# Weight slabs ahead of constants at the start, and the next sample's keys turned in one place, in a hybrid streaming step on one core

## What is computed

```
proj = h @ w_in                         # q, k, v, and the indexer's qi, ki, wi
logits = q @ keys.T * ATTN_SCALE + bias + mask      # 512 cached keys and 16 new ones
probs = softmax(logits)
out = probs @ vals                      # 16 heads, 4 key heads, head size 64
x = x + out @ w_o
```

## Time and profile before

| | us |
|---|---|
| median of 3 runs | 1809.35 (1809.22 to 1810.82) |
| the profiled execution, its own time | 1810.91 |
| its span in the profile | 1809.1 |
| TensorE busy (matmul row) | 1786.6 |
| VectorE busy | 1313.3 |
| ScalarE busy | 825.8 |
| GpSimd busy | 348.8 |

### The profile page before, as it was taken

One profiled execution on the slowest core, in us unless ns is written; L12 is line 12 of the kernel. 1 busy time (PEld: TensorE's weight loads), 2 busy tenths in 40 slices (PEclk: granted clock), 3 DMA queues, 4 the chain that ended last, 5 costly groups with the idle time before them and its releaser, 6 DMA issues.

```text
span 1809.1 us, 35107 instructions
## 1 busy us (share of the span) xinstructions
PE 1786.6 (99%) x13025; PEld 1692.4 (94%) x13025; DVE 1313.3 (73%) x2450; ACT 825.8 (46%) x1477; POOL 348.8 (19%) x381
## 2 busy tenths in 40 slices
PE   8999999999999999999999999999999999999998
PEld 7887668999999999999999999998999999999998
DVE  5498976468576677978788888888535756758786
ACT  4223875334343433536545655456333434334353
POOL 0002663200000000123333343422020100000011
PEclk9999999999999999999999999999999999999999
DMA  6372144333343343233444334444323433334232
GB/s 162 75 121 66 61 135 136 97 87 88 90 95 91 77 111 77 69 79 108 140 138 141 105 122 124 145 139 153 119 81 97 97 94 82 100 82 97 77 84 76
DMA packets 326708, 186.27 MB, mean 103 GB/s; under 512 B 39536, under 2 KB 319184, under 8 KB 325552
## 3 DMA queue, kind: packets, MB, share of 16 engines
q1 hardware_dynamic: 307904, 173.49, 34.1%
q0 software_dynamic: 15840, 7.87, 3.5%
q10 hardware_dynamic: 2832, 3.15, 0.5%
HBM read 164.30 MB, written 19.99 MB: 102 GB/s over the span
## 4 chain that ended last, share of the span: by engine, by line
PE 81%; DVE 3%; ACT 1%; issue 1%; DVEq 0%; ACTq 0%
PE psum L1452 26%; PE psum L203 26%; PE psum L1517 19%; PE psum L621 1%; PE psum L625 1%; PE psum L572 1%; PE psum L585 1%; PE psum L2759 1%; PE psum L554 0%; PE psum L597 0%; PE psum L608 0%; DVE WL L195 0%; PE psum L2730 0%; PE psum L2743 0%; PE psum L566 0%
## 5 line engine op out<-in xcount | busy, mean ns | idle before, releaser
L203 PE MATMUL psum<-b2H,WH 128*128 128x320 f32 x896 | 213.7, 320 | 1.2 <-DVE b2L L1250 0.7
L1517 PE MATMUL psum<-HH,HT 128*128 128x320 f32 x680 | 210.4, 309 | 0.8 <-DVE xT L1731 0.4
L1517 PE MATMUL psum<-HL,HT 128*128 128x320 f32 x680 | 210.7, 310 | 0.0
L203 PE MATMUL psum<-b2H,WL 128*128 128x320 f32 x896 | 204.1, 309 | 0.0
L203 PE MATMUL psum<-b2L,WH 128*128 128x320 f32 x896 | 203.8, 308 | 0.0
L1452 PE MATMUL psum<-b2H,HT 128*128 128x320 f32 x816 | 186.1, 309 | 0.0
L1452 PE MATMUL psum<-b2L,HT 128*128 128x320 f32 x816 | 186.1, 309 | 0.0
L191 ACT ACTIVATE WH<-W 128x1024 fp32r<-128x1024 f32 x89 | 94.0, 1056 | 194.3 <-PE psum L203 180.8
L1517 PE MATMUL psum<-HH,LT 128*128 128x320 f32 x560 | 173.5, 310 | 0.0
L203 PEld LDWEIGHTS psum<-b2H,WH 128*128 128x128 f32 x896 | 146.3, 188 | 11.2 <-issue 8.4
L1452 PE MATMUL psum<-b2H,LT 128*128 128x320 f32 x672 | 153.1, 309 | 0.0
(11 more groups left out here) (437 smaller groups left out, 4203.2 us busy)
## 6 DMA issues: line engine op xcount, KB each, us to landing
W<-ssm_w_in SPq DMA_DIRECT2D x96, 256.0 KB, 3.1
RW<-mlp_w_up SPq DMA_DIRECT2D x64, 256.0 KB, 3.0
RWx<-mlp_w_up SPq DMA_DIRECT2D x64, 256.0 KB, 3.2
RW<-mlp_w_down SPq DMA_DIRECT2D x64, 256.0 KB, 3.1
RWx<-mlp_w_down SPq DMA_DIRECT2D x64, 256.0 KB, 3.2
bc<-scratch_acs SPq DMA_DIRECT2D x8, 1280.0 KB, 7.7
W<-attn_w_in SPq DMA_DIRECT2D x32, 256.0 KB, 3.8
prev<-state_ssm SPq DMA_DIRECT2D x16, 512.0 KB, 5.3
```

The lines of the kernel that those rows point to most:

```text
L203: last = pe.matmul(psum[0:m, b.out + h, 0:TH], w[:, b.slot, k, 0:m], r[:, k, h * TH:(h + 1) * TH], start=(n == 0 and i == 0), stop=(n == K ...
L1517: last = pe.matmul(down_bank(g, i), w[:, k], x[:, DNB[i], k], start=(opens and k == 0 and c == 0), stop=(k == 3 and c == 2), skip_group_ch ...
```

## The change

It has two parts. On SyncE's queue the loads of slab 0 and slab 1 move up behind the first two small loads, then the queue waits until the last column group of the tokens has landed (`x_in[3]`), and only then issues the constants that stood around the slabs.

In the sample streams half 1 of the keys leaves its place between the two halves of the probabilities of step b - 1, and is turned right behind half 0, at the end of step b - 2. It uses bank 5 in place of bank 6, and waits for the copy of the turned probabilities that lay there (`ptn`). VectorE's copy of half 1 (`sample_keys`) moves from behind `sample_turned` to the place between `sample_max` and `sample_normalize`. Every `turn_probs(b, 1)` but the last waits for the copies of the keys of sample b + 1.

```
     def keys_bank(b, a):
-        return 4 + a if b == 0 else 5 if (b, a) == (1, 1) else 6
+        return 5 if a else 6 if b else 4
...
+            load_slab(sp, Block(0), slab_g1(0))
+            load_slab(sp, Block(1), slab_g1(1))
+            sp.wait_ge(x_in[3], 32)
             sp.dma_start(oh_stage[:], A["c_onehot"]).then_inc(c_in, 16)
...
-            load_slab(sp, Block(0), slab_g1(0))
...
-            load_slab(sp, Block(1), slab_g1(1))
             load_slab(sp, Block(2), slab_g1(2))
...
-                elif b >= 1:
-                    pe.wait_ge(ske, 2 * b + (1 if b > 1 else 0))
+                elif b:
+                    pe.wait_ge(ptn, 2 * b - 2) if b > 1 else pe.wait_ge(ske, 2)
...
-                elif g_is_first(b):
-                    pe.wait_ge(ske, 4)
+                elif not b_is(b, DB - 1):
+                    pe.wait_ge(ske, 2 * b + 4)
...
                 if not g_is_first(b):
                     turn_sample_heads(b - 1)
-                if not last and b:
-                    turn_keys(b + 1, 1 - s, i + s, 1)
                 turn_probs(b, 1)
...
                 if not last and not b_is(b, DB - 2):
                     turn_keys(b + 2, s, i + 1, 0)
+                    turn_keys(b + 2, s, i + 1, 1)
...
                 sample_turned(b)
                 last = b_is(b, DB - 1)
-                if not last and b:
-                    sample_keys(b + 1)
...
                     sample_max(b + 1, 0)
                     sample_max(b + 1, 1)
+                if b + 2 < DB:
+                    sample_keys(b + 2)
                 sample_normalize(b)
```

## The result

The changed kernel takes 1814.28 us (median of 8 runs, 1813.78 to 1814.95), the kernel before 1809.24 us in the same comparison (8 runs, 1808.83 to 1810.82). The ratio is 1.0026, 95% interval 1.0017 to 1.0035: slower by 5.0 us, 0.28%, and more than the 0.2% that can be told. The forecast was 1814.0.

A forecast was written before the change was run, and what follows sets the result against it. TensorE, busy 99% of the span, was taken as the bound, with the streams a ring of four engines. Streams +5.0 and opening -0.4 gave +4.6 us, from 1809.35 to about 1814.0; 8-in-10 range 1809.0 to 1815.7.

The forecast's parts named there:

- The streams: Sample streams: VectorE's key copy delays normalization, heads and weighing by 0.83 us a step, 5.0 us over six streams.
- What was costed at nothing: Sample streams: moving TensorE's four half-1 transposes costs 0; the new waits for key copies and bank 5 end early enough.
- the 0.36 us of idle time ahead of the first probabilities: Sample streams: TensorE's wait before the first probabilities, into which the moved half-1 transposes fall, at cost 0.
- The opening: Start of the kernel: slab waits saved against later tokens, -0.4 us in sum, between -1.3 and +0.7.
- the 0.3 that was taken: Opening: tokens come later as slabs compete for full DMA engines, 0.3 us of a range of 0 to 0.7.
- The second term: Opening: some 0.2 us of later waits on slab 0's low part would go.
- the rival on TensorE's pace: Opening: TensorE reaches its quick pace by 11.5 instead of 15.4 us, 1.6 us less, 1812.4; chance 0.2.
- the loss of 0.7 us: Opening: by the rule of interleaving loads alone, the full loss of 0.7 us, making the sum 1815.1.
- The -1.3 for the opening: Opening: the fastest bound given for its -0.4 us; the other bound was +0.7.
- the forecast's own range: Whole kernel: 1811.9 to 1815.7, from streams 4.2 to 5.7 us longer and opening -1.3 (-2.0 with early quick pace) to +0.7.
- The last rival: Sample streams: TensorE's pace falls to that of the opening, 18 us more in all, 1832; chance 0.03.
- The constants: Opening: the nine constant loads moved back land by about 23 us, before TensorE wants them at 27.52.

The follow-up runs named there:

- the run with ScalarE's new order: Changed kernel with VectorE's key copy behind the normalization, plus ScalarE's exponentials ahead of its key copy and first tail ahead of the heads: 1808.65 us, ratio 0.9992.
- the run with the opening alone: Kernel before with only SyncE's queue changed (slabs 0 and 1 ahead, constants behind the last tokens): 1809.76 us, ratio 1.0001.
- the last two experiments: Kernel with ScalarE's and VectorE's new stream orders, plus slab 0's low part split before chunk 2's copy: 1808.06 us; or plus the old load order: 1808.42 us.

## Why the prediction was right, step by step

**The streams: right in mechanism, place and nearly in size.** The forecast said that the copy would start at 1.75 us behind the first maximum, that TensorE would stand near 0.9 us ahead of the heads, and that ScalarE's copy of them and the weighing would be 0.83 us late. The profile has 1.76, 0.89, 0.79 and 0.81 us. The step came out at 6.40 to 6.42 us instead of 6.49, and the six streams at 4.45 instead of 5.0 us. The difference lies behind the weighing, where the forecast let nothing be taken back: before, the maximum started straight behind VectorE's low part of the heads' tile, 2.02 us after the weighing; in the changed kernel it starts on the logits, 1.95 us after it. Before, that second chain, which the run with ScalarE's new order then laid open, was the later one by 0.07 us; in the changed kernel it no longer is.

**What was costed at nothing was nothing.** The transposes of half 1 moved on TensorE, bank 5, and the wait of the second probabilities for the copies: the kernel with the copy behind the normalization has all of them and takes the time of the kernel before. It also shows why the 0.36 us of idle time ahead of the first probabilities could be filled without a gain: the second ones wait for ScalarE all the same.

**The opening: near in number, by luck.** The forecast was -0.48 - 0.2 + 0.3 = -0.4 us. The wait for slab 0 did go, but it gave only 0.07 us at the first products (11.43 for 11.50), since the tokens came late in its place: chunks 2 and 3 started 0.77 us later (0.49 in the run with the opening alone), above the 0.3 that was taken and beyond the range of 0 to 0.7. The second term didn't come: the low part's products started at 12.76 in both profiles, as VectorE's split stands behind its copy of chunk 2, and that copy now came late with the tokens. At 14.32 us the two profiles are level; the loads have given nothing and cost nothing. What the profile has gained at the constants' products, 0.2 us, comes from the rival on TensorE's pace, which had a chance of 0.2. The kernel before:

```profile
14.32 0.73 PE L203 MATMUL psum<-b1L,WH 128*128 128x320 f32 x2
```

And the changed kernel:

```profile
14.32 0.49 PE L203 MATMUL psum<-b1L,WH 128*128 128x320 f32 x2
...
14.93 0.71 PE L2504 MATMUL psum<-cst,x_stage 128*128 128x128 f32 x5
```

The quick pace began at about 14.4 us in place of 15.2, not at 11.5 as the rival had it. The next five transposes started 0.46 us earlier (14.93 for 15.39), and later waits took back half of it. So the small gain is luck. It isn't shown that the change caused it: the granted clock reads 1.00 from 5 to 20 us in both profiles, and the pace turned at about 12 us in one profile with the new order and at 15.1 in another. In the times the opening is worth 0.0 us (-1.4 to +1.8).

The rule of the Trainium skill that was weighed there ("DMA: Bandwidth & Descriptors", section "Issuing engines are not separate DMA queues"), that loads from both queues interleave on the same engines, agrees with the profiles: the tokens' second group, issued at 2.45 as before, was there at 9.4 instead of 8.6. Over all profiles TensorE starts on it at 8.0 to 8.6 us with the old order and at 9.1 to 10.0 with the new one. That delay didn't become the loss of 0.7 us that was worked out beside the rule, since the slab's wait was gone.

Two bounds of the forecast don't follow from its terms. The -1.3 for the opening has no row behind it: with no delay of the tokens the terms give -0.7. And the lower end of the forecast's own range, with the early pace, is 1809.35 + 4.2 - 2.0 = 1811.55, not 1811.9. The last rival, a slower pace of TensorE in longer steps, didn't come: eight transposes took 1.09 us in the changed streams, as they had ahead of the streams before.

**The constants** were covered, as forecast: their products never waited for a load.

**The sum.** 4.6 us were forecast; 4.2 us is what the two profiles show from 300 to 1801 us, and 5.0 us (interval 3.1 to 6.3) the times. The profiled execution was forecast to have a span of 1813.7 and had 1812.5: 0.4 us of that is the difference of 4.6 and 4.2, and 0.8 us is time that the kernel before had lost at its end and the changed kernel had not (below). What is left between 4.2 and 5.0 us is within the interval and was not traced further.

## What to carry to other kernels

In a ring of engines that are all busy most of the time, an instruction moved on one engine is judged by what stands directly behind it and by who waits for that, not by its own length: a copy of 0.69 us that needed nothing sooner, put ahead of a normalization on whose result TensorE, ScalarE and TensorE again wait in turn, cost about 0.75 us in each of six steps, and two instructions further down it cost nothing. Filling an engine's idle time with work gains nothing where the next wait ends on another engine: the step fell when the order on the engines that set it was changed, from 5.65 to 5.46 us with ScalarE's and to 5.35 with VectorE's as well. And here, with the DMA engines full (357 GB/s), the weight slab that was brought forward was paid for by the tokens that it crowded: they came 0.5 to 2.0 us later in every profile with the new order, while the slab itself was begun on at 9.1 to 10.8 us in place of 9.6 to 10.4.

## What the runs showed of the hardware that was not expected

The last stage, 27 transposes of the output, takes 4.81 us in some executions and 3.14 us in others of the same code. The timeline of the kernel before, and its windows (the last three figures are PEclk, the DMA share and GB/s):

```profile
1799.74 4.81 PE L1924 MATMUL psum<-cst,y_fin 128*128 128x128 f32 x27
```

```profile
1795.00:1799.00 4.00, 2.85 (x22) 2.59 (x20) 1.84 (x8) 0.80 (x3) 0.00 (x0) 1.00 0.00 0
1799.00:1801.00 2.00, 1.92 (x16) 1.95 (x17) 1.72 (x5) 1.18 (x2) 0.00 (x0) 0.90 0.11 43
1801.00:1805.00 4.00, 3.56 (x19) 3.31 (x17) 1.79 (x3) 1.52 (x2) 0.00 (x0) 0.63 0.94 372
```

And of the changed kernel:

```profile
1803.92 3.14 PE L1924 MATMUL psum<-cst,y_fin 128*128 128x128 f32 x27
```

```profile
1799.00:1803.00 4.00, 3.02 (x23) 2.76 (x21) 1.67 (x8) 0.62 (x2) 0.00 (x0) 1.00 0.00 0
...
1805.00:1809.00 4.00, 2.06 (x19) 1.82 (x17) 2.27 (x4) 1.80 (x2) 0.00 (x0) 1.00 1.02 407
```

The granted clock fell from full speed (2.4 GHz) to a mean of 0.63 between 1801 and 1805 us, that is for most of that stretch to the lower level of 1.2 GHz, in the kernel before, after a stretch in which TensorE had been busy 2.85 of 4.00 us; it stayed at 1.00 in the changed kernel, after 3.02 of 4.00 us. That busy time doesn't tell the two ends apart: the profile of the opening alone had 2.77 of 4.00 us from 1795 to 1799 and kept 1.00. What decides it these runs don't show. Of the eleven profiles four have the slow end (4.81 us): the kernel before, the copy ahead in every other stream, and the last two experiments; the other seven have 3.14 us. Only a part of these 1.7 us reaches the span, as the output's stores, which fill the DMA engines (a share of 1.02 in the last row), end behind them: from the start of the 27 transposes to the end of the span it is 8.5 to 8.6 us in the seven and 9.1 to 9.8 us in the four, so the slow end costs 0.5 to 1.3 us. In the pair shown here it is 0.8 us: 4.2 us apart at the start of the transposes, 3.4 us in the spans. That is part of the spread of the 8 runs of the kernel before (1808.83 to 1810.82) and more than the opening of this study is worth. Two profiles are therefore compared stage by stage, not by their spans.

The openings differ from execution to execution too: with the old order of the loads the constants' products started at 27.52, 27.07 and 27.32 us, with the new one between 27.03 and 27.59 (28.44 with the low part of slab 0 first).
